# RWKV scan: inverted blocks in a 64-row buffer with zeros, unit matrices in turn, another order of the pair work

## Chip, cores, metric

One core of a Trainium2 chip runs one program of two transformer blocks in float32. The metric is the device time of that program in microseconds (us). The change touches one stage of it, the bidirectional RWKV scan, which takes about a quarter of the time.

## What is computed

The scan keeps, for each of 16 heads and 2 directions, a 64 x 64 state `s` and walks over 512 tokens (256 of context, then 256 of the sequence):

```python
def step(s, inp):
    r_t, lw_t, k_t, v_t, a_t, b_t = inp
    sa = jnp.einsum('dbhij,dbhj->dbhi', s, a_t)
    s = s * jnp.exp(lw_t)[..., None, :] + sa[..., None] * b_t[..., None, :] + v_t[..., None] * k_t[..., None, :]
    return s, jnp.einsum('dbhij,dbhj->dbhi', s, r_t)
```

The kernel does this in 16 chunks of 32 tokens. Inside a chunk the term `sa` depends on earlier tokens of the same chunk; it is solved with the inverse of a unit triangular 32 x 32 matrix. So for every head, direction and chunk there is one 32 x 32 inverse, and then a 64 x 64 matrix that takes the state from one chunk to the next.

## The kernel before, in words

The stage is `stage_rwkv_scan`. Eight **head pairs** n = 0 to 7 (two heads e = 0, 1 of 64 channels fill the 128 partitions) pass through it in a software pipeline. `scan_order()` writes one list of items by hand; all engines walk the same list, each taking its part of each item, and each engine works strictly in that order. For i = -3 to 8 it interleaves: the chain of pair i, the solve of pair i+1, the grams of pair i+2, the readout of pair i-1, the bonus and inverse of pair i+2 and the preparation of pair i+3. `interleave` gives each group a window (lo, hi) of the period; items are spread evenly in their window and then sorted. I call the time from one chain start to the next **a period**. Tiles are named by the items:

- `el`, `gram`, `btok`: VectorE makes the scaled inputs (L1915 to L1920, six operations on 128 x 512); TensorE multiplies them to 64 x 64 grams (L1581), VectorE masks them into BG (L1968); TensorE turns the inputs to token order (L1589), ScalarE copies them out.
- `inv`: SyncE writes the grams' 32 x 32 blocks (partitions 32 to 63 and 96 to 127 of BG, columns 96 to 127) to DRAM (L1503) and reads them back with one block per partition (L1510, L1512); VectorE inverts them in 30 double operations (L1933, L1935) and a last one (L1940); SyncE writes the inverses to DRAM (L1517) and reads them back into the same place of BG (L1521).
- `atok`, `akv`, `pq`, `gr`: the solve. `atok` transposes (L1589, copy L1851). `akv` (`key_values`, L1599) multiplies 32-row blocks. `pq` (`solved`) copies four blocks through TensorE with a 32 x 32 unit matrix (L1611: partitions 0 to 31 and 64 to 95) and multiplies the inverses with the values (L1618: partitions 32 to 63 and 96 to 127, output in the same ones); ScalarE copies the bank back (L1866). `gr` (`steps_made`) first lays unit matrices (L1634) and the read vectors (L1636) into two banks, for e = 0 and then e = 1, and adds products on them (L1641).
- `chain` c = 0 to 16: per chunk L1660, L1653, L1668, L1677 on TensorE, then one VectorE operation (L1987) that scales the state U for the next chunk. Chunk 1 of a pair also waits until VectorE has summed the pair before (L1999, L2000; item `read` 0).
- `kk`, `lora`, `scan`, `exps`: the preparation of pair i+3. `kk` 0 starts with a square on ScalarE (L1808), whose input SyncE loads (L1487, L1488) after `bonus` of the pair before is done on VectorE (L1979).

TensorE runs each float32 matmul as two passes, so a matmul of the code has two records in the trace. The items up to the first half of a period are, before, in this order (pair 3 in the chain): el 5/0, atok 4/0, chain 0, read 0, gram 5/0, atok, exps 5/1, akv, chain 1, read 1, btok, akv, chain 2, btok, read 2, pq, el 5/1, pq, chain 3, read 3, gram 5/1, pq, btok, pq, chain 4, read 4, btok, gr, bonus, chain 5, gr.

Of the kernel before, what the change touches and what calls it, by code (L numbers as in the profile page):

```python
# [20 lines left out]
P = 128  # L21
D = 1024
T = 256
KT = D // P
# [1314 lines left out]
def scan_order():  # L1339

    order = []
    for i in range(-3, KT + 1):
        def has(n, x):
            return x if 0 <= n < KT else []
        order += interleave((0, 1, has(i, [("chain", i, c) for c in range(NCK + 1)])),
                            (0, 0.7, has(i + 1, scan_solve(i + 1))),
                            (0, 0.3, has(i + 2, scan_grams(i + 2))),
                            (0, 0.3, has(i - 1, scan_read(i - 1))),
                            (0.3, 0.36, has(i + 2, [("bonus", i + 2, j) for j in range(2)])),
                            (0.45, 1, has(i + 2, [("inv", i + 2, s) for s in range(1, LCH)])),  # L1350
                            (0.42, 1, has(i + 3, scan_ready(i + 3))))
    return order


def stage_rwkv_scan(nc, k, a, lora, kept, o):
# [14 lines left out]
    with ExitStack() as ctx:  # L1370
# [37 lines left out]
        starts, gmask, sel, half2 = sb("starts", 512), sb("gmask", 64), sb("sel", 512), sb("half2", 6)  # L1408
        cen, omka, eps = sb("cen", P), sb("omka", KT), sb("eps", 1)
# [4 lines left out]
        x_kept = [nc.dram_tensor(f"rw_{s}_kept", (P, KT * T), F32) for s in ("x", "ctx")]  # L1414
        consts, step = sem("consts"), sem("step")
# [42 lines left out]
        with nc.Block() as block:  # L1458
# [8 lines left out]
            @block.vector  # L1467
            def _(dve):
                nc.vector.memset(er.rearrange("p (c s) -> p c s", s=LCH)[:, :, LCH - 1], 1.0)
                nc.vector.memset(en.rearrange("p (c s) -> p c s", s=LCH)[:, :, LCH - 1], 1.0)  # L1470
                nc.vector.memset(eps, GN_EPS)
                kas = row(k, "rw", 0, 9 * KT).rearrange("p (n j) -> p n j", j=9)[:, :, KA]
                nc.vector.tensor_scalar(omka, kas, -1.0, 1.0, ALU.mult, ALU.add)
                nc.vector.scalar_tensor_tensor(cen, headones, -1.0 / 64, ident, ALU.mult, ALU.add)
# [4 lines left out]
        def _(sp):  # L1479
# [19 lines left out]
            for n in range(KT):  # L1499
# [18 lines left out]
                sp.wait_ge(x_out, 32 * (n + 1))  # L1518
                for d in range(2):
                    for h in range(2):  # L1520
                        sp.dma_start(BG[n % 3][d][brows(h), :, :, 96:128].rearrange("p c e t -> p (c e) t"),  # L1521
                                     blocks(mt_dram, n, d, h)).then_inc(mt_in, 16)
# [12 lines left out]
        def _(pe):  # L1535
# [68 lines left out]
            def solved(n, d, e, half):  # L1604
# [8 lines left out]
                for j in range(4):  # L1613
                    c2 = 4 * half + j
                    for h in range(2):
                        x, y = VQ[n % 2][d][brows(h), c2, e, :], KP[d][brows(h), c2, e, :]
                        both = bass.AP(x.tensor, x.offset, [list(x.ap[0]), [y.offset - x.offset, 2], [1, 64]])
                        mm = pe.matmul(out[brows(h), j * P:(j + 1) * P], BG[n % 3][d][brows(h), c2, e, 96:128], both,  # L1618
                                       start=True, stop=True)
# [3 lines left out]
            def steps_made(n, d, half):  # L1623
# [4 lines left out]
                for h in range(2):  # L1628
                    for e in range(2):
                        unit = ident[rows64(e), rows64(e)]  # L1630
                        to = outs[h][rows64(e), 0:384].rearrange("p (c v) -> p c v", c=4)
                        rt = RT[n % 2][d][rows64(e), 256 * half:256 * half + 256].rearrange("p (c h t) -> p c h t", h=2,
                                                                                           t=LCH)
                        pe.matmul(to[:, :, 0:64], unit, unit.unsqueeze(1).to_broadcast([64, 4, 64]), start=True, stop=False,  # L1634
                                  skip_group_check=True)
                        pe.matmul(to[:, :, 64:96], unit, rt[:, :, h, :], start=False, stop=False, skip_group_check=True)  # L1636
# [962 lines left out]
```

## Time and profile before

| | us |
|---|---|
| median of 3 runs | 2722.91 (2720.7 to 2728.16) |
| the profiled execution | 2720.06 |
| its span, first to last instruction | 2718.4 |
| TensorE busy | 2245.3 (83%) |
| VectorE busy | 984.4 (36%) |
| ScalarE busy | 518.1 (19%) |
| mean granted share of the TensorE clock | 0.858 |

The page cuts the span into 40 slices of 68 us; the scan lies in slices 25 to 35. The views used are the page, busy time by windows, the timelines of single engines, and the answers for single lines. In a timeline a row is a run of equal instructions: start, duration, engine, line, operation, output and inputs, tile form (rows*columns of the array, then the moving operand) and count, and in brackets the idle time before it and what ended it. The granted clock takes two values in the scan, 0.50 (1.2 GHz) and 1.00 (2.4 GHz).

### The profile page before, as it was taken

To read this page: it belongs to the slowest core of one execution; us is meant where nothing else is said; L and a number is where in the kernel's file an instruction comes from. 1 tells how busy PE (TensorE), PEld (TensorE's weight loads), DVE (VectorE), ACT (ScalarE), POOL (GpSimd) and SP (SyncE) were. 2 spreads that over 40 slices of the span, in tenths; PEclk is the share of its full clock that TensorE was granted. 3 is DMA by queue.
4 is the path that set the end of the run, shared out by engine and by line. 5 is a ranking of instruction groups with operands and counts; after the bars stand their busy time and mean duration, and the time that the engine had idled before them with its cause. 6 is when DMAs were issued, how large, how long until landed. Compare 5 with 4: busy or idle time off the path is not lost. (4 is left out here: it accounts for less than half of the span.)

```text
span 2718.4 us, 39159 instructions
## 1 busy us (share of the span) xinstructions
PE 2245.3 (83%) x16630; PEld 1735.0 (64%) x16630; DVE 984.4 (36%) x2209; ACT 518.1 (19%) x920; POOL 58.2 (2%) x85
## 2 busy tenths in 40 slices
PE   1999955798999886899859993688888889779797
PEld 0888854687888775788624442466666777536445
DVE  3224346411440372675161003544544441120253
ACT  1011022401000101100110003444444333010142
POOL 0000000000000300000000000000000000000000
PEclk9999977898999898899979995776667776689889
DMA  7465410424874321775303203111101111312100
GB/s 289 173 230 228 171 64 8 86 93 165 336 280 155 124 78 37 281 302 217 138 16 109 92 31 125 38 39 38 35 15 39 29 25 41 124 66 93 52 10 16
DMA packets 103014, 305.14 MB, mean 112 GB/s; under 512 B 71352, under 2 KB 79800, under 8 KB 85184
## 3 DMA queue, kind: packets, MB, share of 16 engines
q1 hardware_dynamic: 94384, 225.11, 24.3%
q0 software_dynamic: 8464, 77.60, 7.3%
q8 instruction: 131, 2.15, 0.3%
q14 instruction: 35, 0.29, 0.0%
HBM read 286.88 MB, written 15.80 MB: 111 GB/s over the span
## 5 line engine op out<-in xcount | busy, mean ns | idle before, releaser
L263 PE MATMUL bank<-h,ring 128*128 128x256 f32 x2944 | 646.7, 383 | 22.8 <-DVEq L967 15.3
L263 PEld LDWEIGHTS bank<-h,ring 128*128 128x128 f32 x2944 | 566.3, 193 | 104.0 <-DVEq L967 16.0
L263 PE MATMUL bank<-mixed,ring 128*128 128x512 f32 x384 | 165.0, 592 | 1.3 <-DVE mixed L1249 1.3
L877 PE MATMUL bank<-ffn_hidden,ring 128*128 128x256 f32 x704 | 152.4, 379 | 3.3 <-PEq L903 3.3
L877 PEld LDWEIGHTS bank<-ffn_hidden,ring 128*128 128x128 f32 x704 | 133.6, 190 | 22.2 <-issue 4.1
L263 PEld LDWEIGHTS bank<-mixed,ring 128*128 128x128 f32 x384 | 72.9, 190 | 93.5 <-issue 91.4
L156 DVE CUSTOM_DVE_ANT_0 next_w<-next_w,next_vec,par 128x1024 f32<-128x1024 f32 x96 | 120.1, 1279 | 11.4 <-DMA next_w<-in_mod_stream 11.4
L1987 DVE TENSOR_TENSOR rw_u<-bank,rw_lam 128x128 f32<-128x128 f32 x120 | 35.0, 291 | 236.1 <-PE bank L1660 233.1
L889 DVE SCALAR_TENSOR_TENSOR x<-bank,mod,x 128x256 f32<-128x256 f32 x24 | 10.0, 477 | 231.6 <-PE bank L877 231.6
L1668 PE MATMUL bank<-rw_gr,rw_u 64*64 64x32 f32 x960 | 80.3, 252 | 13.0 <-DVE rw_u L1987 12.9
L1581 PE MATMUL bank<-rw_xa,ring 64*64 64x64 f32 x1024 | 30.5, 305 | 72.2 <-DVE rw_xa L1920 72.2
L877 PE MATMUL bank<-y,ring 128*128 128x256 f32 x384 | 83.1, 379 | 0.8 <-PEq L679 0.8
L401 DVE COPY y<-bank 128x512 f32<-128x512 f32 x20 | 13.8, 692 | 186.2 <-PE bank L263 186.2
L877 PEld LDWEIGHTS bank<-y,ring 128*128 128x128 f32 x384 | 72.9, 190 | 10.9 <-issue 1.1
L2087 PE MATMUL bank<-mla_h,ring 128*128 128x256 f32 (+1 forms) x240 | 67.3, 444 | 12.5 <-PEq L190 12.5
L1581 PEld LDWEIGHTS bank<-rw_xa,ring 64*64 64x64 f32 x1024 | 27.6, 212 | 75.6 <-DVE rw_xa L1920 74.5
L1090 DVE SCALAR_TENSOR_TENSOR cv_v<-cv_u,par,cv_v 128x256 f32<-128x256 f32 x150 | 67.4, 483 | 22.1 <-DVE cv_v L1090 21.0
L1668 PEld LDWEIGHTS bank<-rw_gr,rw_u 64*64 64x64 f32 x960 | 66.5, 172 | 13.9 <-issue 13.5
L1677 PE MATMUL bank<-ring 64*64 64x32 f32 x768 | 69.4, 261 | 0.5
L1660 PE MATMUL bank<-rw_u,rw_gr 64*64 64x64 f32 x896 | 61.8, 270 | 8.3 <-DVE rw_u L1987 5.6
L2087 PEld LDWEIGHTS bank<-mla_h,ring 128*128 128x128 f32 x240 | 46.6, 195 | 33.1 <-issue 28.1
L962 ACT ACTIVATE ffn_gate<-bank 128x512 f32<-128x512 f32 x22 | 13.1, 597 | 286.0 <-PE bank L263 286.0
(387 smaller groups left out, 3415.1 us busy)
## 6 DMA issues: line engine op xcount, KB each, us to landing
ring<-in_stream SPq DMA_DIRECT2D x89, 2048.0 KB, 8.0
next_w<-in_mod_stream POOLq DMA_DIRECT2D x24, 2048.0 KB, 9.9
ctx<-in_mod_rest POOLq DMA_DIRECT2D x16, 1024.0 KB, 7.3
rwkv_projections<-proj_out POOLq DMA_DIRECT2D x8, 1024.0 KB, 6.7
y<-bias_table SPq DMA_DIRECT2D x48, 128.0 KB, 4.9
rw_rkv<-rwkv_projections SPq DMA_DIRECT2D x8, 768.0 KB, 4.2
rw_at<-rw_at_kept SPq DMA_DIRECT2D x16, 256.0 KB, 3.9
rwkv_o<-rwkv_projections POOLq DMA_DIRECT2D x1, 2048.0 KB, 16.0
```

What stands on the lines that cost most here:

```text
L156: return nc.vector.tensor_tensor_reduce(products, w, vec, 1.0, bias, ALU.mult, ALU.add, out)
L263: mm = pe.matmul(out, ring_tile(k, n, kt, i * P), rhs[kt], start=start and kt == kts[0], stop=stop and kt == kts[-1])
L401: nc.vector.tensor_copy(dst, k.psum[2 * (j % 2)].rearrange("p (i t) -> p i t", i=2)).then_inc(stored_dve, 1)
L877: mm = pe.matmul(k.psum[grp * 4 + i][:, 0:T], ring_tile(k, n, kt, i * P), rhs[part * KT + kt], start=(part == 0 and kt == 0), stop=(part = ...
L962: nc.scalar.activation(gate[:, j % 2, :], k.psum[2 * (j % 2)][:], ACT.Silu).then_inc(gated, 1)
L1090: nc.vector.scalar_tensor_tensor(v[:, i:i + 1, :], u[:, i:i + 1, bass.ds(t * U + j, T)], k.par[:, bass.ds(t * U + (PAR["dw"] + i * (TAPS + ...
L1581: mm = pe.matmul(outs[e][rows64(c % 2), 64 * (c // 2):64 * (c // 2) + 64], BK[rows64(e), c].rearrange("p k s -> p (k s)"), both, start=Tru ...
L1660: mm = pe.matmul(k.psum[c % 2][rows64(e), 64 * d:64 * d + 64], GR[n % 2][d][rows64(e), c, 0:64], U[rows64(e), c % 2, d, :], start=False, s ...
L1668: mm = pe.matmul(k.psum[2 + c % 2][rows64(e), at:at + 32], U[rows64(e), c % 2, d, :], GR[n % 2][d][rows64(e), c, 64:96], start=(d == 0), s ...
L1677: mm = pe.matmul(k.psum[2 + h][rows64(e), at:at + 32], VQ[n % 2][d][rows64(h), c2, e, :], BG[n % 3][d][rows64(h), c2, e, 64:96], start=(c ...
L1987: v.tensor_tensor(U[:, (c + 1) % 2, :, :], k.psum[c % 2][:, 0:P].rearrange("p (d v) -> p d v", d=2), lam[:, n % 4, :, c + 1:c + 2].to_broa ...
L2087: mm = pe.matmul(out, ring_tile(k, n, kt, i * P), rhs[kt], start=(kt == 0), stop=(kt == KT - 1))
```

## The change

It has four parts. (1) The inverses come back from DRAM into a buffer of their own, LM, in which the partitions 0 to 31 and 64 to 95 are zeros, written once; L1618 then multiplies 64 rows (a tile of 64 x 32) in place of 32. SyncE waits for all `pq` of the pair before it writes LM. (2) In `gr` the unit matrices are fed for e = 0 and e = 1, then the read vectors for both. (3) `scan_order` has other windows. (4) The mask and `cen` move into constants that this stage no longer needs otherwise, which makes room for LM.

```diff
-                            (0, 0.7, has(i + 1, scan_solve(i + 1))),
-                            (0, 0.3, has(i + 2, scan_grams(i + 2))),
+                            (0, 0.75, has(i + 1, scan_solve(i + 1))),
+                            (0.1, 0.42, has(i + 2, scan_grams(i + 2))),
                             (0, 0.3, has(i - 1, scan_read(i - 1))),
-                            (0.3, 0.36, has(i + 2, [("bonus", i + 2, j) for j in range(2)])),
-                            (0.45, 1, has(i + 2, [("inv", i + 2, s) for s in range(1, LCH)])),
-                            (0.42, 1, has(i + 3, scan_ready(i + 3))))
+                            (0.42, 0.46, has(i + 2, [("bonus", i + 2, j) for j in range(2)])),
+                            (0.55, 1, has(i + 2, [("inv", i + 2, s) for s in range(1, LCH)])),
+                            (0.48, 0.9, has(i + 3, scan_ready(i + 3))))
...
+                for d in range(2):
+                    for h in range(2):
+                        nc.vector.memset(LM[d][krows(h)].rearrange("p a b t -> p (a b t)"), 0.0)
...
+                if n:
+                    sp.wait_ge(pq_up, 8 * n)
...
-                        sp.dma_start(BG[n % 3][d][brows(h), :, :, 96:128].rearrange("p c e t -> p (c e) t"),
+                        sp.dma_start(LM[d][brows(h)].rearrange("p c e t -> p (c e) t"),
...
-                        x, y = VQ[n % 2][d][brows(h), c2, e, :], KP[d][brows(h), c2, e, :]
+                        x, y = VQ[n % 2][d][rows64(h), c2, e, :], KP[d][rows64(h), c2, e, :]
...
-                        mm = pe.matmul(out[brows(h), j * P:(j + 1) * P], BG[n % 3][d][brows(h), c2, e, 96:128], both,
-                                       start=True, stop=True)
+                        mm = pe.matmul(out[brows(h), j * P:(j + 1) * P], LM[d][rows64(h), c2, e, :], both, start=True,
+                                       stop=True)
...
+                    for e in range(2):
+                        pe.matmul(to[e][:, :, 0:64], units[e], units[e].unsqueeze(1).to_broadcast([64, 4, 64]), start=True,
+                                  stop=False, skip_group_check=True)
+                    for e in range(2):
...
+                        pe.matmul(to[e][:, :, 64:96], units[e], rt[:, :, h, :], start=False, stop=False,
                                   skip_group_check=True)
```

The new order of a period, with TensorE's items in the same words: atok 4/0, chain 0, (read 0 on VectorE), atok, chain 1, read 1, akv, (el 5/0), akv, chain 2, read 2, gram 5/0, pq, (exps 5/1), chain 3, pq, read 3, btok, pq, btok, chain 4, read 4, pq, (el 5/1), gr, chain 5, gram 5/1, gr, btok, chain 6, atok 4/1, btok, bonus, atok, chain 7, (bonus on VectorE), akv, chain 8, akv, kk 0, pq, lora, chain 9, pq, kk 1, chain 10, pq, pq, lora, chain 11, gr, kk 2, gr, chain 12 to 16.

## Rows read from the trace of the kernel before

**Rows 1.** The page: the span, and the granted clock in 40 slices.
```profile
span 2718.4 us, 39159 instructions
PEclk9999977898999898899979995776667776689889
```
**Rows 2.** Windows: one period, then stretches of it; from:to, length, busy us, clock, DMA.
```profile
2007.40:2089.30 81.90, 71.12 (x1167) 57.58 (x1166) 38.18 (x110) 32.93 (x58) 0.00 (x0) 0.69 0.15 33
2018.88:2029.82 10.94, 10.94 (x116) 9.15 (x115) 0.58 (x2) 6.38 (x12) 0.00 (x0) 0.50 0.01 1
2018.88:2039.65 20.77, 20.77 (x275) 17.08 (x274) 6.15 (x12) 8.79 (x17) 0.00 (x0) 0.50 0.01 2
2039.65:2056.72 17.07, 15.29 (x303) 12.19 (x301) 5.31 (x10) 6.11 (x12) 0.00 (x0) 1.00 0.45 111
2056.72:2066.96 10.24, 10.24 (x110) 7.75 (x112) 3.04 (x15) 3.49 (x6) 0.00 (x0) 0.50 0.01 2
```
**Rows 3.** TensorE's timeline at the head of the next period (chain 0 to chain 1).
```profile
2089.30 0.72 PE L1653 MATMUL bank<-ring 64*64 64x64 f32 x16
2095.24 1.99 PE L1581 MATMUL bank<-rw_xa,ring 64*64 64x64 f32 x64 [5.21 <-DVE rw_xa L1920]
...
2098.94 1.92 PE L1599 MATMUL bank<-ring,x 32*32 32x64 f32 x32 [0.68 <-ACT ring L1851]
```
**Rows 4.** VectorE's timeline over the same head.
```profile
2086.15 0.29 DVE L1987 TENSOR_TENSOR rw_u<-bank,rw_lam 128x128 f32<-128x128 f32 x1
2090.96 0.37 DVE L1940 TENSOR_SCALAR rw_x<-rw_x 64x16 f32<-64x16 f32 x2
2094.49 0.69 DVE L1920 SCALAR_TENSOR_TENSOR rw_xa<-rw_kk,rw_ee 128x512 f32<-128x512 f32 x1
2096.66 0.42 DVE L2000 TENSOR_TENSOR rw_ysb<-rw_ysb,bank 128x256 f32<-128x256 f32 x1
```
**Rows 5.** TensorE's timeline: other idle times of a period, kk 2, and the tail.
```profile
2046.99 1.13 PE L1706 MATMUL bank<-ring,con 128*128 128x512 f32 x2 [0.84 <-DVE ring L1973]
2056.65 1.84 PE L1553 MATMUL bank<-rw_half,rw_bb 128*128 128x2 f32 x8 [0.26 <-ACT rw_bb L1808]
2079.26 1.15 PE L1559 MATMUL bank<-rw_kstT,rw_sel 8*128 8x128 f32 x8
2082.86 0.69 PE L1660 MATMUL bank<-rw_u,rw_gr 64*64 64x64 f32 x8 [0.82 <-DVE rw_u L1987]
2086.59 0.49 PE L1668 MATMUL bank<-rw_gr,rw_u 64*64 64x32 f32 x5 [2.23 <-DVE rw_u L1987]
```
**Rows 6.** Timelines: bonus (VectorE), square (ScalarE), last readout operation, exponents; then L1488's landing.
```profile
2048.75 0.68 DVE L1979 TENSOR_TENSOR rw_bonv<-bank,rw_rkv 128x512 f32<-128x512 f32 x1
2055.88 0.72 ACT L1808 ACTIVATE rw_bb<-rw_rkv,par 128x512 f32<-128x512 f32 x1
2044.80 0.75 DVE L2012 SCALAR_TENSOR_TENSOR rwkv_o<-rw_ycs,par,rwkv_o 128x512 f32<-128x512 f32 x1
2098.78 0.62 ACT L1791 COPY rw_xa<-rw_rkv 128x512 f32<-128x512 f32 x1
2102.38 0.80 ACT L1798 ACTIVATE ring<-rw_av,rw_omka,par 128x512 f32<-128x512 f32 x1
DMA to landing us min/median/max: 4.2/5.0/7.9
```
**Rows 7.** TensorE's timeline: a pq at the low clock, then one at the full clock.
```profile
2062.11 0.63 PE L1611 MATMUL bank<-ring,con 32*32 32x256 f32 x2
2062.12 0.64 PE L1618 MATMUL bank<-ring 32*32 32x128 f32 x4
2069.69 0.41 PE L1611 MATMUL bank<-ring,con 32*32 32x256 f32 x2
2069.94 0.82 PE L1618 MATMUL bank<-ring 32*32 32x128 f32 x12
```
**Rows 8.** TensorE's timeline: transposes, then the unit matrices of gr, at the full clock.
```profile
2043.18 0.66 PE L1589 MATMUL bank<-con,ring 128*128 128x128 f32 x4
2043.76 0.66 PE L1634 MATMUL bank<-con 64*64 64x256 f32 x4
```
**Rows 9.** TensorE's timeline: the first gram in the two periods that fill the pipeline.
```profile
1718.19 1.99 PE L1581 MATMUL bank<-rw_xa,ring 64*64 64x64 f32 x64 [16.72 <-DVE rw_xa L1920]
1777.61 1.99 PE L1581 MATMUL bank<-rw_xa,ring 64*64 64x64 f32 x64 [13.45 <-DVE rw_xa L1920]
```

More of the change, by code:

```diff
@@ L1407, in stage_rwkv_scan @@
         U, lam = sb("u", 2, 2, 64), sb("lam", 4, 2, NCK)
-        starts, gmask, sel, half2 = sb("starts", 512), sb("gmask", 64), sb("sel", 512), sb("half2", 6)
-        cen, omka, eps = sb("cen", P), sb("omka", KT), sb("eps", 1)
+        starts, gmask, sel, half2 = sb("starts", 512), const(k, "tri")[:, 0:64], sb("sel", 512), sb("half2", 6)
+        cen, omka, eps = const(k, "neg"), sb("omka", KT), sb("eps", 1)
         kst, kstT, rst, rstT = sb("kst", 8), sb("kstT", P), sb("rst", 8), sb("rstT", P)
@@ L1414, in stage_rwkv_scan @@
         x_kept = [nc.dram_tensor(f"rw_{s}_kept", (P, KT * T), F32) for s in ("x", "ctx")]
+        LM = [sb(f"lm{d}", 8, 2, LCH) for d in range(2)]
         consts, step = sem("consts"), sem("step")
@@ L1628, in steps_made @@
                 for h in range(2):
+                    to = [outs[h][rows64(e), 0:384].rearrange("p (c v) -> p c v", c=4) for e in range(2)]
+                    units = [ident[rows64(e), rows64(e)] for e in range(2)]
                     for e in range(2):
-                        unit = ident[rows64(e), rows64(e)]
-                        to = outs[h][rows64(e), 0:384].rearrange("p (c v) -> p c v", c=4)
+                        pe.matmul(to[e][:, :, 0:64], units[e], units[e].unsqueeze(1).to_broadcast([64, 4, 64]), start=True,
+                                  stop=False, skip_group_check=True)
+                    for e in range(2):
                         rt = RT[n % 2][d][rows64(e), 256 * half:256 * half + 256].rearrange("p (c h t) -> p c h t", h=2,
                                                                                            t=LCH)
-                        pe.matmul(to[:, :, 0:64], unit, unit.unsqueeze(1).to_broadcast([64, 4, 64]), start=True, stop=False,
+                        pe.matmul(to[e][:, :, 64:96], units[e], rt[:, :, h, :], start=False, stop=False,
                                   skip_group_check=True)
-                        pe.matmul(to[:, :, 64:96], unit, rt[:, :, h, :], start=False, stop=False, skip_group_check=True)
                 for j in range(4):
```

## The prediction

> **What bounds the kernel now.** I read the page first, then busy time by windows, then the timelines of TensorE, VectorE and ScalarE over one period. The page says that the clock of TensorE is near full in most of the program but 0.6 to 0.7 in the slices of the scan [rows 1]. The windows then show one period: 81.90 us, of which TensorE is busy 71.12 us and VectorE only 38.18 us [rows 2]. So TensorE is the bound, with 10.8 us idle, and it is slowed by its clock: between chain 1 and chain 7 it works 20.77 us at clock 0.50 (1.2 GHz), then 17.07 us at 1.00 (2.4 GHz), then 10.24 us at 0.50 again [rows 2]. The periods of pairs 2 to 5 are alike within 0.1 us; those of pairs 0 and 1 have larger gaps at their start [rows 9]. Five periods (chain of pairs 0 to 4) have all the groups of the list in them, so a change per period counts five times, and the rest is worked out apart.
>
> Most of the 10.8 us lies in four places. At the head of a period TensorE waits 5.21 us for VectorE's inputs of the first gram, and 0.68 us for ScalarE's copy before akv [rows 3]; before the bonus 0.84 us, before kk 0 0.26 us [rows 5]; the second akv has the same 0.68 us; and at the tail chain 14 and 15 wait 0.82 and 2.23 us for VectorE [rows 5], which is busy there with inverse and scans. At that head VectorE itself is never idle: after the state of chunk 15 (2086.15) it ends the inverse at 2091.33, the gram's inputs at 2095.18, and the sum of the readout at 2097.08 [rows 4].
>
> **Part 1: the order.** *Head.* Chain 1 comes 2098.94 + 1.85 = 2100.79 today, 14.6 us after the state of chunk 15 was scaled [rows 3, 4]. In the new list VectorE does, after the inverse (2091.33), the state of chunk 1 (0.3) and the readout sum (1.6), then chain 1 may start at about 2093.3, some 7.2 us after 2086.15. TensorE does the second atok before it; gram (1.92), first akv (1.85 and its wait of 0.68) come later, which are 4.45 us that it still has to do, less the wait. So the gain is 14.6 - 7.2 - 4.6 = 2.8 us. The waits before the bonus and the second akv go, since chain steps or transposes now stand between: 0.8 and 0.7 us. The gram's inputs, now made under akv, akv and chain 2, are no longer late.
>
> *Tail.* kk 2 (1.08 us of progress, [rows 5]) stood between chain 12 and 13. VectorE's work between the states of chunks 13 and 15 stays at 7.4 us or so (four inverse steps and a scan each), so without kk 2 TensorE only idles longer: +1.1 us.
>
> *New waits.* (a) kk 0. The load for it is released by the bonus on VectorE, which moves from before chain 5 to behind chain 7. Today the bonus operation ends at 2049.43, 1.4 us after its chain step starts, and the square runs at 2055.88 with the landing median 5.0 us after issue [rows 6]. So kk 0 can start 1.4 + 0.5 + 5.0 + 0.7 = 7.6 us after chain 7 starts at worst, about 7.3 by the spacing of the earlier pairs; TensorE has chain, akv, chain, akv in between, 4.1 us at the full clock, 7.4 us at the low one. Stalls 3.2 us instead of 0.26: +2.9 us. Behind it stand pq and lora on TensorE. (b) The second gram. VectorE now does the three readout operations (2.2 us, the last in [rows 6]) before the six inputs (4.1 us; they end at 2095.18, [rows 4]), both after read 4 on TensorE, which meanwhile has only pq, gr and chain 5, 4.5 us: +1.7 us at the full clock, none at the low one. (c) ScalarE's exponents take 2098.78 to 2103.18 = 4.4 us [rows 6] and now stand between two pq copies; the second btok needs the bank of the second: 0 to 1 us, I take 0.8. Sum of the order without clock: -2.8 - 1.5 + 1.1 + 2.9 + 1.7 + 0.8 = +2.2 us per period. By itself the new order is no gain.
>
> **Part 2: the padded blocks.** A pq today runs its two kinds of matmul side by side: at the low clock L1618 starts 0.01 us after L1611, though that takes 0.63 us a pass, and the whole block costs 1.86 us, at the full clock 1.01 [rows 7]. That works as they use different partitions. The padded L1618 uses partitions 0 to 127, so also those of L1611, though other output columns. Lower bound: it still runs beside, 0 us. Upper bound: L1618 waits for both passes of L1611, 2 x 0.43 at the low clock (2 x 0.24 at the full one) plus a change of form, for which the nearest row is four transposes, 0.11 us apart: the next form starts 0.58 us after the first, not 0.44, so about 0.1 [rows 8]. That makes +0.5 at the full clock and +1.0 at the low one; with six blocks at full and two at low, 5.0 us per period, of which 1.4 us fill waits (b) and (c): +3.6. No row has two forms at work at once, which speaks for the upper end; the row in which both kinds overlap speaks for the lower [rows 7]. I take the middle, +1.8, and keep both ends. The Trainium skill has a rule that speaks against the change: "TensorEngine Tiling (Array Packing)", Tiling Modes, says that a switch of the tiling mode, not only of the tile, drains the array. By it the sum would go to the upper end; the trace agrees in that a new form starts late [rows 8].
>
> **Part 3: the clock.** At the low clock a pq costs 1.86 us, at the full one 1.01 [rows 7]. What TensorE did before the clock rose at 2039.65: the second gram (64-row tiles, four of them), then pq; before 2066.96: pq and lora with 64 x 128 tiles. In between, with 32-row pq, akv, chain steps and the small sums, it stayed at 0.50 though TensorE was busy all the time [rows 2]. In the new order the first gram follows chain 2 and read 2 without idle time and is followed by padded pq, so I expect the rise after it, not after the second. Low-clock work from chain 1 to there: 10.94 us today up to the first pq [rows 2], less two btok (2.1), plus the second akv and the gram (1.85 + 1.92): 12.6, plus one pq. The second low stretch becomes kk 0 and a pq, some 4.7 us. Against 20.77 + 10.24 + 3.8 (gram and akv, moved in) = 34.8 now, 20.3: 14.5 us fewer at the low clock; such work takes 1/1.8 of the time at full, so -6.4 us per period. Bounds: 0 if nothing lifts it, -8.5 if the second low stretch goes as well.
>
> **Part 4: no cost.** Unit matrices in turn: today the four passes of L1634 already span 0.66 us for two halves, and at 256 columns a pass of one half takes 0.21, so two passes of both halves side by side take 0.43 plus the end of the last; both halves are at work together [rows 8]. Gain 0 to 0.1 us for each of 32 gr; I take 0. The memsets (four, at most 0.7 us) lie beside the loads of constants. The wait of SyncE for pq of the pair before: those end long before the inverse does; behind it only the return of the inverses is queued.
>
> **Sum.** Per period 2.2 + 1.8 - 6.4 = -2.4 us, five times: -12. The period of pair 5 (no kk): -3. The filling periods: TensorE stood idle 16.72 and 13.45 us before the first gram [rows 9]; atok and two akv now go into the first (5.4 us, until the first pq waits for the inverses: -3.6), and the second gains 1 us more than a later one. Last periods: padded pq against an earlier clock, 0. Total -19.6, on the profiled 2720.06: 2700.5; the median of the runs is 2.9 us higher, so **2703 us**, 0.7% less.
>
> **Rivals.** *A. The padded blocks run beside the copies.* Then -4.2 per period, and the low clock of pair 6's period is shortened as well (-5): -21 - 5 - 4.6 - 5 = -36, and up to -10 more if the clock is kept at kk 0: 2676 to 2687, say 2682. For it: other output columns. Chance 0.22. *B. The drain of the skill's rule in full, as priced from [rows 7, 8].* 2.2 + 3.6 - 6.4 = -0.6 per period, +4 in the pairs around, -4.6 at the start: -4, so 2719. Chance 0.18. *C. Slower.* The clock stays low through the first direction. Then the gain of 6.4 is gone, six pq at the low clock and two at full pay 7.0, waits (b) and (c) vanish: -4.3 + 1.1 + 2.9 + 7.0 = +6.7 per period, +33 in all, with start and end +32: 2755. It decides at the first gram and the pq behind it: is 1.00 granted before chain 4? For it: today a gram (1.99 us) at the head of the period is followed by 25 us at 0.50. Against it: it came after 5.21 us of idle time [rows 3]. Chance 0.20. *Forecast:* 0.40.
>
> **Numbers.** The range goes to A's low end and some more below, and part of the way to C: 2660 to 2738. A measurement of this kernel tells about 0.3% (8 us) from none. Faster: the forecast nearly whole (0.37), A (0.22): 0.59. Within: B and the rest of the forecast, 0.20. Slower: C and a little, 0.21.
>
> **What would show it.** Head: the wait before chain 1 about 3 us, none before the first gram. A row L1553 with 2 to 3.5 us of idle time before it. In pq, the start of L1618 against L1611: 0.01 us (A) or 0.5 us and more (B). The clock of the 20 us after chain 1: rise some 15 us in. Period 79 to 80 us. The forecast fails if the load is not late, if ScalarE becomes what TensorE waits for, or if the clock rises only with the second gram.

## The result, and the profile after

The changed kernel takes 2730.61 us (median of 20 runs, 2724.92 to 2736.34), the kernel before 2720.76 us in the same comparison. The ratio is 1.0036, with a 95% interval of 1.0027 to 1.0045: slower by 0.36% or 10 us, just beyond the 0.3% that the prediction called none. The forecast was 2703 us, and faster. The time lies within the stated range, but on the other side of the kernel before.

The profiled execution took 2728.41 us, 8.35 us more than the one of before. The page of the changed kernel, its span and the granted clock in slices (compare [rows 1]: in the scan, slices 28, 29 and 32 to 34 went up):

```profile
span 2726.8 us, 39174 instructions
PEclk9999977998999898999979995777867887689889
```

Busy time by windows, the columns of [rows 2]: the period of pair 3, then its low-clock stretch after chain 1, the full-clock stretch, and the low-clock stretch behind it.

```profile
2018.48:2101.17 82.69, 68.44 (x1167) 52.16 (x1167) 38.20 (x110) 33.88 (x58) 0.00 (x0) 0.79 0.16 32
2022.57:2037.81 15.24, 15.24 (x220) 12.29 (x222) 5.87 (x11) 3.81 (x6) 0.00 (x0) 0.50 0.19 30
2037.81:2065.10 27.29, 24.39 (x517) 19.07 (x513) 10.88 (x20) 12.53 (x24) 0.00 (x0) 1.00 0.31 65
2065.10:2075.40 10.30, 6.90 (x39) 3.99 (x41) 0.63 (x4) 4.19 (x6) 0.00 (x0) 0.50 0.09 30
```

The mean granted clock went from 0.69 to 0.79, and TensorE is busy 68.44 us instead of 71.12 [rows 2]. Yet the period is 0.8 us longer. So the change did bring the clock that it was forecast to bring, and paid more than that for it. TensorE's timeline of the same period shows where: the head (compare [rows 3]), the first gram, a block of `pq` at the full clock, the second btok and the second gram, kk 0, a block of `pq` at the low clock (compare [rows 7]), and the tail (compare [rows 5]).

```profile
2018.48 0.72 PE L1661 MATMUL bank<-ring 64*64 64x64 f32 x16
2022.57 0.55 PE L1668 MATMUL bank<-rw_u,rw_gr 64*64 64x64 f32 x5 [2.32 <-DVE rw_ysb L2008]
...
2033.58 1.99 PE L1587 MATMUL bank<-rw_xa,ring 64*64 64x64 f32 x64
...
2039.15 0.62 PE L1617 MATMUL bank<-ring,con 32*32 32x256 f32 x4
2039.70 1.06 PE L1624 MATMUL bank<-ring,rw_lm 64*32 64x128 f32 x16
...
2043.71 0.63 PE L1595 MATMUL bank<-con,ring 128*128 128x128 f32 x4 [0.76 <-ACT ring L1874]
...
2052.56 1.16 PE L1587 MATMUL bank<-rw_xa,ring 64*64 64x64 f32 x64 [1.23 <-DVE rw_xa L1928]
...
2068.50 1.87 PE L1559 MATMUL bank<-rw_half,rw_bb 128*128 128x2 f32 x8 [4.22 <-ACT rw_bb L1816]
2070.30 1.06 PE L1617 MATMUL bank<-ring,con 32*32 32x256 f32 x4
2071.29 1.92 PE L1624 MATMUL bank<-ring,rw_lm 64*32 64x128 f32 x16
...
2094.64 0.45 PE L1668 MATMUL bank<-rw_u,rw_gr 64*64 64x64 f32 x8 [2.58 <-DVE rw_u L1995]
...
2098.45 0.50 PE L1676 MATMUL bank<-rw_gr,rw_u 64*64 64x32 f32 x5 [2.92 <-DVE rw_u L1995]
```

The head: 2.32 us before chain 1 and none before the gram, in place of 5.21 and 0.68. A `pq`: L1624 starts 0.55 us after L1617 (2039.70 - 2039.15) at the full clock and 0.99 us after it at the low one, where L1618 started 0.01 us after L1611 at the low clock [rows 7]. All four passes of the two copies end first, then the 16 passes of the eight products run. The two numbers are the same in all 58 of the 64 blocks that lie wholly at one clock. From the start of the copies to the start of what follows, a block takes 1.54 us at full and 2.84 us at low clock (the full width 0.55 + 1.06 less the 0.07 us by which neighbours overlap), before 1.01 and 1.86.

TensorE's idle time and its low-clock time per period, as a mean over the periods of pairs 1 to 4, worked out from the same timelines, in us:

| | period | TensorE busy | idle | granted 0.50 |
|---|---|---|---|---|
| before | 81.90 | 71.13 | 10.77 | 51.2 |
| after | 82.97 | 68.58 | 14.38 | 35.2 |

So 16.0 us per period were moved from the low clock to the full one, busy time fell by 2.55 us only, and idle time rose by 3.6: kk 0 +4.24, tail +2.3, second gram +1.23, second btok +0.76, against -5.1 at the head and before akv and bonus. The four periods give +4.3 us of the 8.35. The first period, which also has all groups, gives +4.8 (84.7 against 79.9), the filling +3.0 (chain 0 of pair 0 at 1766.72 instead of 1763.68). The last two periods and what follows them give 3.7 back (-0.5 and -0.7 for the periods of pairs 5 and 6).

Why kk 0 is late is read on three engines. First VectorE's timeline, the bonus that releases the loads:

```profile
2060.79 0.68 DVE L1987 TENSOR_TENSOR rw_bonv<-bank,rw_rkv 128x512 f32<-128x512 f32 x1
```

Then SyncE's own queue, the last of the reads of the inverse's inputs and the two loads:

```profile
2059.34 0.60 SPq L1516 DMA_DIRECT2D rw_x<-rw_at_kept  x1
2061.56 0.34 SPq L1491 DMA_DIRECT2D rw_rkv<-rwkv_projections  x1
2061.94 0.57 SPq L1492 DMA_DIRECT2D rw_w<-in_lora_out  x1
```

ScalarE's timeline, the square:

```profile
2067.72 0.72 ACT L1816 ACTIVATE rw_bb<-rw_rkv,par 128x512 f32<-128x512 f32 x1 [2.81 <-DMA rw_w<-in_lora_out]
```

And the answer for line L1492, from issue to landing in all 8 pairs:

```profile
DMA to landing us min/median/max: 5.2/5.8/7.2
```

The bonus ends at 2061.47, the loads are issued at 2061.56 and 2061.94, the second lands 5.76 us later, and the square starts at once. TensorE has nothing between 2064.3 and 2068.50. The clock also falls in this wait, at 2065.10, and stays down for the 10.30 us of the last window. The load that ScalarE waits for is the one for the lora weights, which the square doesn't use: the wait is on both loads at once.

The bonus is not the only thing that holds the loads back. SyncE issues them behind the reads of the inverse's inputs, in one queue. In the period of pair 2 the bonus ended at 1976.41, and the load followed the last of these reads. SyncE's queue there:

```profile
1976.24 0.60 SPq L1516 DMA_DIRECT2D rw_x<-rw_at_kept  x1
1977.02 0.52 SPq L1491 DMA_DIRECT2D rw_rkv<-rwkv_projections  x1
```

This is the period in which kk 0 waits longest, 5.96 us.

The filling periods, TensorE's timeline of the changed kernel (compare [rows 9]):

```profile
1707.58 3.62 PE L1605 MATMUL bank<-ring 32*32 32x64 f32 x64 [8.07 <-ACT ring L1859]
1715.90 1.99 PE L1587 MATMUL bank<-rw_xa,ring 64*64 64x64 f32 x64 [4.70 <-DVE rw_xa L1928]
1719.30 1.06 PE L1617 MATMUL bank<-ring,con 32*32 32x256 f32 x4 [1.41 <-DMA rw_lm<-rw_mt_kept]
...
1747.22 1.87 PE L1559 MATMUL bank<-rw_half,rw_bb 128*128 128x2 f32 x8 [7.16 <-ACT rw_bb L1816]
```

The akv did move into the idle time before the first gram, but that gram starts at 1715.90 instead of 1718.19 [rows 9], where VectorE's inputs set it; and kk 0 of pair 2 waits 7.16 us, 1.30 us before the change.

### The profile page after: what moved, and what is told of

Read it like the earlier page. It is cut to its first block and busy times, and to the rows that moved or that the text cites. A ratio compares the mean times of both kernels' runs of the same rounds, so it can differ in the third digit from the quotient of the medians.

```text
span 2726.8 us, 39174 instructions
## 1 busy us (share of the span) xinstructions
PE 2240.8 (82%) x16630; PEld 1706.8 (63%) x16630; DVE 986.8 (36%) x2213; ACT 521.4 (19%) x924; POOL 58.2 (2%) x85
## 5 line engine op out<-in xcount | busy, mean ns | idle before, releaser
L1676 PE MATMUL bank<-rw_gr,rw_u 64*64 64x32 f32 x960 | 74.5, 242 | 15.3 <-DVE rw_u L1995 15.2
L1668 PEld LDWEIGHTS bank<-rw_u,rw_gr 64*64 64x64 f32 x896 | 42.1, 158 | 71.8 <-issue 64.8
L1624 PEld LDWEIGHTS bank<-ring,rw_lm 64*32 64x32 f32 x1024 | 58.4, 121 | 36.9 <-issue 33.6
L1624 PE MATMUL bank<-ring,rw_lm 64*32 64x128 f32 x1024 | 81.2, 307 | 0.0
L1676 PEld LDWEIGHTS bank<-rw_gr,rw_u 64*64 64x64 f32 x960 | 61.0, 160 | 16.1 <-issue 15.8
```

What stands on the lines that cost most here:

```text
L1624: mm = pe.matmul(out[brows(h), j * P:(j + 1) * P], LM[d][rows64(h), c2, e, :], both, start=True, stop=True)
L1668: mm = pe.matmul(k.psum[c % 2][rows64(e), 64 * d:64 * d + 64], GR[n % 2][d][rows64(e), c, 0:64], U[rows64(e), c % 2, d, :], start=False, s ...
L1676: mm = pe.matmul(k.psum[2 + c % 2][rows64(e), at:at + 32], U[rows64(e), c % 2, d, :], GR[n % 2][d][rows64(e), c, 64:96], start=(d == 0), s ...
```

## The experiments

Each kernel was compared with the kernel before on the same chip. The theories at the outset: **F**, the change of tile form inside a block makes L1624 wait for L1617; **S**, not the form but the shared partitions make it wait; **L**, the late loads behind the bonus cost the gain; **O**, the order is a loss by itself. Ratios are to the kernel before, with the 95% interval.

**1. The padded blocks alone (e1_pad_only).** Old windows, old order in `gr`:

```diff
-                            (0, 0.75, has(i + 1, scan_solve(i + 1))),
-                            (0.1, 0.42, has(i + 2, scan_grams(i + 2))),
+                            (0, 0.7, has(i + 1, scan_solve(i + 1))),
+                            (0, 0.3, has(i + 2, scan_grams(i + 2))),
...
```

> The kernel before with the padded blocks alone (LM buffer, 64-row L1618, the wait for pq before LM is written), old order, old gr. Theory (the padded block waits for the copies' passes and a change of form): a pq takes 1.54 us at the full clock and 2.84 us at the low one, as in the changed kernel, against 1.01 and 1.86 before; +4 to +5 us per period, of which an earlier rise of the clock gives back some; 2720 to 2740 us. Rival (the padding is free and lifts the clock, the loss is the order's): faster than before, 2700 us or less.

Measured: 2721.7 us, ratio 1.0007 (0.9998 to 1.0016). Period 80.79 us, low-clock time 34.7 us against 51.2, blocks at 1.54 and 2.84 us. The time lies in the range of the theory, but the period is 1.1 us shorter and not longer. In this one profile the low-clock time falls from 42.5 to 26.6 us over the four periods; steadier is the mean granted clock of whole runs, 0.872 to 0.877 in all 11 against 0.850 to 0.867 in the 76 runs of the kernel before that were made beside the experiments. So the clock rises by the padding without any new order, and the longer blocks eat it.

**2. The order alone (e2_order_only).** The kernel before with the six new windows.

> The kernel before with the new windows of the order alone; blocks of 32 rows, old gr. Theory: the same waits as in the changed kernel (2.3 us before chain 1, 0.8 before the second btok, 1.2 before the second gram, about 4 before kk 0), pq at 1.01 us; the clock rises later than in the changed kernel, since the first gram is followed by 32-row blocks. 2715 to 2735 us. Rival (the order alone lifts the clock, the padding only costs): clock rises within 16 us after chain 1, 78 us per period, 2705 us or less.

Measured: 2734.56 us, ratio 1.0058 (1.0041 to 1.0075). Period 85.57, low-clock time 54.0: the new order doesn't lift the clock, and costs 14 us. Its waits are near those of the changed kernel: chain 1 2.32, kk 0 3.95 in the mean (2.4 to 6.4), chain 14 and 15 2.58 and 2.35. The second gram waits 1.72 us in two of the four periods and not at all in the other two, and the second btok does not wait.

**3. The turn alone (e3_turn_only), and the same kernel again (e3_turn_again).**

```diff
-                        pe.matmul(to[:, :, 0:64], unit, unit.unsqueeze(1).to_broadcast([64, 4, 64]), start=True, stop=False,
+                        pe.matmul(to[e][:, :, 0:64], units[e], units[e].unsqueeze(1).to_broadcast([64, 4, 64]), start=True,
...
```

> The kernel before with the unit matrices fed to both halves in turn alone. Theory: both halves were at work together before; 0 to -0.1 us for each of 32 gr, so 2718 to 2721 us. Rival (they were serial): -0.4 us each, -13 us.

> The unit matrices in turn alone, once more, for a second profile. Its times fell into two groups, 2707 to 2714 and 2735 to 2743 us. Theory (the same work, locked in two ways to the changes of the clock): a profile of either group has the same durations at each clock and the same waits, and differs in the time spent at the low clock; in the slow group a period takes 3.4 us more or twice that. Rival (contention for memory or a late load): a wait appears in the slow group that the other has not.

Measured: 2726.98 us (12 runs, from 2706.61 to 2742.77), ratio 1.0027 (0.9995 to 1.0058); again, 2730.76 us (5 runs), ratio 1.0049 (1.0027 to 1.007). Neither is the 2718 to 2721 us of the theory. Of the first 12 runs five lie at 2707 to 2714 and seven at 2727 to 2743, with nothing between. Windows over the period of pair 3, of a profiled run of the first group, then of one of the second:

```profile
2003.43:2081.93 78.50, 66.68 (x1167) 53.92 (x1166) 38.21 (x110) 32.83 (x58) 0.00 (x0) 0.74 0.17 34
```
```profile
2004.99:2086.91 81.92, 70.89 (x1167) 57.49 (x1166) 38.20 (x110) 32.95 (x58) 0.00 (x0) 0.69 0.15 33
```

The same instructions, with the same waits (0.4 us more at each of chain 14 and 15 in the first), but at clock 0.74 and 0.69. Each repeats its period over pairs 1 to 4 within 0.03 us. That the other runs of a group have the same rhythm as its profiled one is inferred from their times alone, and no run of this kernel above 2728 us was profiled. The turn itself is worth some 0.05 us per `gr`: at the full clock it takes 2.29 to 2.32 us before, from its start to the start of what follows, and 2.23 to 2.27 with the turn.

**4. One form of tile in the block (e4_one_form).** The changed kernel, with the copy multiplying 64 rows too; the unit matrix has zeros in the rows of the inverse, so its result is the same:

```diff
-                              ident[krows(h), krows(h)], VQ[n % 2][d][krows(h), at, e, :], start=True, stop=True)
+                              ident[rows64(h), krows(h)], VQ[n % 2][d][rows64(h), at, e, :], start=True, stop=True)
```

> The changed kernel, but the four copies of pq also take 64 rows (a 64 x 32 slice of the unit matrix), so that both kinds of matmul in a pq have the same tile form, with other output columns. Theory (the change of form makes L1624 wait): without it they run side by side, pq near 1.05 us at full and 1.9 us at the low clock, some -4 us per period, 2705 us. Rival (the shared partitions make it wait): pq stays at 1.45 us and more, 2726 us or more.

Measured: 2703.72 us, ratio 0.9939 (0.9926 to 0.9952). TensorE's timeline, a block at the full clock and the start of one at the low clock:

```profile
2033.76 0.41 PE L1617 MATMUL bank<-ring,con 64*32 64x256 f32 x2
2033.78 0.41 PE L1624 MATMUL bank<-ring,rw_lm 64*32 64x128 f32 x4
2034.00 0.38 PE L1617 MATMUL bank<-ring,con 64*32 64x256 f32 x2
2034.02 0.82 PE L1624 MATMUL bank<-ring,rw_lm 64*32 64x128 f32 x12
```
```profile
2030.08 0.64 PE L1617 MATMUL bank<-ring,con 64*32 64x256 f32 x2
2030.09 0.64 PE L1624 MATMUL bank<-ring,rw_lm 64*32 64x128 f32 x4
```

Copies and products now read all the same partitions, and still L1624 starts 0.01 or 0.02 us after L1617. The block costs 1.01 and 1.86 us, as before the change. F holds, S falls: the row range of one matmul's operands is worth 27 us. What stays untested is whether two forms would run side by side if they also read different partitions.

**5 to 7. The loads earlier.** The lora weights (L1492) are loaded a pair ahead and the first two planes of rkv before the bonus; only the third plane stays behind it, with a semaphore of its own. On the changed kernel (e5_early_load), on the one with one form (e6_one_form_early), and on the kernel before with the new order (e8_order_early):

```diff
-                    sp.wait_ge(lora_up, 2 * n)
-                    sp.wait_ge(bon_down, n)
-                sp.dma_start(rkv, kept[n, :, 0:3, :]).then_inc(loaded, 16)
-                sp.dma_start(w2, a["lora_out"][:, :, n * P:(n + 1) * P]).then_inc(loaded, 16)
+                sp.dma_start(rkv[:, 0:2, :], kept[n, :, 0:2, :]).then_inc(loaded, 16)
+                if n >= 1:
+                    sp.wait_ge(bon_down, n)
+                sp.dma_start(rkv[:, 2, :], kept[n, :, 2, :]).then_inc(v_loaded, 16)
+
+            def load_w(n):
+                if n >= 1:
+                    sp.wait_ge(lora_up, 2 * n)
+                sp.dma_start(w2, a["lora_out"][:, :, n * P:(n + 1) * P]).then_inc(loaded, 16)
...
```

> The changed kernel with the load that kk 0 waits for taken apart: L1492's weights a pair ahead, the first two thirds of L1491 without the wait for the bonus, the last third behind it. Theory (the late bonus makes kk 0 wait about 4 us, the first cost of the new order): the wait before kk 0 falls to 1.3 to 2.5 us, some -2 to -3 us per period and more in the filling periods (7 and 8 us there), so -12 to -20 us against the changed kernel: 2710 to 2718 us, just under the kernel before. Rival (the stall only takes the place of other idle time or of low-clock time): no change, 2728 to 2732 us.

> Both mends: one tile form in pq and the load taken apart. Theory (two separate costs, both on TensorE's path): they add up, 2704 - 12 to 20 = 2684 to 2692 us. Rival (they share idle time or clock): 2698 to 2706 us, as with one form alone.

> The new order alone, 32-row blocks, with the load taken apart. Theory (the order costs by its stalls, most by that of kk 0): 2734 falls by 12 to 20 us to 2714 to 2722 us, near the kernel before; the clock stays low longer than in the changed kernel. Rival (the order costs by the clock, not by the load): 2728 us or more.

Measured: 2724.05 us, ratio 1.0016 (1.0002 to 1.0031); 2697.27 us, ratio 0.9922 (0.9893 to 0.9951); 2728.94 us, ratio 1.0036 (1.0018 to 1.0055). That is 6.6, 6.4 and 5.6 us less than the same kernels without it, about half of the 12 to 20 us of the theories; only the first is clear of the noise, as the intervals of the others overlap with those of the kernels without it. The third time lies in the range of its rival. The wait before kk 0 falls from 4.5 to 3.3, from 4.8 to 3.3 and from 3.95 to 1.8 us per period. Why it does not go is seen in SyncE's queue, here of e5_early_load:

```profile
2060.15 0.60 SPq L1524 DMA_DIRECT2D rw_x<-rw_at_kept  x1
2060.86 0.67 SPq L1489 DMA_DIRECT2D rw_rkv<-rwkv_projections  x1
```

The load no longer waits for the bonus (which ends at 2062.35) but follows the last read of the inverse's inputs by 0.7 to 0.8 us, as it does for every pair but the first in all three kernels. These reads wait for the second gram, which the new order also moved. Issued ahead of the reads the load could go earlier; no run tried it. L is a part of the loss, some 6 of the 9 to 14 us that the order costs.

**8. One form, old order (e7_one_form_old_order), and with the turn (e9_one_form_turn).** The edit of experiment 4 on the kernel of experiment 1, and the same with the turn.

> The padded blocks with one tile form, in the old order and with the old gr. Theory (padding without the change of form is free and the clock rises earlier): pq 1.0 us at full and 1.9 at the low clock, low-clock time per period some 12 us shorter than before, 2695 to 2705 us. Rival (the clock gain came from the new order, not from the padding): 2715 to 2722 us.

> Padded blocks with one tile form in the old order, and the unit matrices in turn. Theory (the turn gains 0.04 us per gr, as its rows in the changed kernel say, and otherwise only moves where the clock changes fall): 2688 to 2696 us, the same as without it, perhaps with two groups of times. Rival (the turn costs, as its median alone seemed to say): 2698 us or more.

Measured: 2692.53 us, ratio 0.9901 (0.9877 to 0.9924); 2691.55 us, ratio 0.9894 (0.9879 to 0.9909). The good part of the change, taken alone, is worth 1%: the blocks cost what they did before the change, and low-clock time falls from 51.2 to 41.0 us per period. Not all of that is owed to the zero rows: the first group of experiment 3 has none and stands at 40.9 us in a period of 78.49, against 78.54 here. But this kernel is 19 us faster than that group (medians 2692.5 and 2711.8), in the first period (74.2 against 81.6 us) and in that of pair 6 (52.3 against 60.0). The new order costs 11 us of it (2703.72 in experiment 4). The turn adds nothing that can be told. O holds with all three kinds of block: the new order costs 14, 9 and 11 us (table below).

**9. Another order (e10_gram_later), and with the early loads (e11_gram_later_early).** From the kernel e7_one_form_old_order, the grams are moved only a little and the bonus stays near its place:

```diff
-                            (0, 0.3, has(i + 2, scan_grams(i + 2))),
+                            (0.07, 0.34, has(i + 2, scan_grams(i + 2))),
...
-                            (0.3, 0.36, has(i + 2, [("bonus", i + 2, j) for j in range(2)])),
+                            (0.34, 0.37, has(i + 2, [("bonus", i + 2, j) for j in range(2)])),
...
-                            (0.42, 1, has(i + 3, scan_ready(i + 3))))
+                            (0.45, 1, has(i + 3, scan_ready(i + 3))))
```

> Padded blocks with one form, old gr, and the old order but for the grams at 0.07 to 0.34, the bonus at 0.34 to 0.37 and the preparation from 0.45: chain 1 before the first gram, but the bonus before chain 6. Theory (of the new order the head is a gain and the late bonus and readout are the loss): 2.3 us of waiting before chain 1 in place of 5.2 and 0.7, no wait before kk 0 over 0.5 us, up to 1 us before the second gram; 3 us per period less, 2675 to 2685 us. Rival (idle time at the head is paid back at the tail or by the clock): 2690 to 2700 us.

> The kernel with the grams at 0.07 to 0.34 and also the load taken apart. Theory (kk 0 does not wait for the load there): the same within 3 us. Rival (it still does, above all in the filling periods): 5 us or more below it.

Measured: 2656.23 us, ratio 0.9767 (0.9754 to 0.9781); 2649.78 us, ratio 0.9744 (0.9731 to 0.9758). Both beat both kernels. The first is 19 us below even the low end of its theory: the waits at the head shrink to 1.4 us, but kk 0 waits 1.6 in place of at most 0.5, and what the text had not reckoned with is the clock, with low-clock time of 25.5 us per period of 71.53. With the early load the rival holds, 6.5 us less, but hardly at the kk 0 of the full periods, where the wait falls only from 1.6 to 1.3: the square there follows ScalarE's copy of the second akv without idle time, so no load is late. The kk 0 of pair 2, in the filling, waits 1.37 us in place of 4.15, and chain 0 of pair 0 comes 4.3 us earlier.

**10. That order with the other two kinds of block (e12_two_forms_gram_later, e13_short_rows_gram_later).** The copy with 32 rows again (the first edit of experiment 4 undone); and the kernel before, with the three windows of experiment 9.

> Order of the kernel with the grams a little later (2656 us with one form of tile), blocks of the changed kernel with their two forms. Theory 'a form change is paid in every block': 128 blocks of 0.53 us at the full clock, as in the old order where the pair of kernels stood 29 us apart, so 2656 + 30 = about 2685. Rival 'the idle times hide it': this order has little idle time behind the blocks, but VectorE's head and tail waits could absorb some; then 2665 to 2675. Rival 'the clock follows': if the form change also takes the clock down in the middle of a period, 2695 or more.

> The same order on the kernel before, with its 32-row blocks and no padding. Theory 'padding lifts the clock': low-clock time per period stays near 45 to 50 us in place of 25.5, so at 1.8 times the work a period of 79 to 81 us and 2700 to 2715 in all. Rival 'the order alone does it': no wait before the first gram and a clock that rises after it, as with padding: period near 72 us, 2660. What decides is the granted clock between chain 1 and chain 4.

(The 128 blocks of the first text should read 64: eight pairs of eight; at 0.53 us they are 34 us.) Measured: 2703.74 us, ratio 0.9937 (0.9908 to 0.9965); 2716.24 us, ratio 0.9957 (0.9934 to 0.9981). The first is 47.5 us slower than with one form, more than 34: "the clock follows". The second is 1 us above the range of its theory and 56 above its rival; its low-clock time (36.7 us) and period (76.0 us) lie between the two, and its periods are uneven, from 72.7 to 80.9 us. With the others this fills a table of medians, which is the shortest statement of what the parts do:

| us | order of before | order of the change | order of experiment 9 |
|---|---|---|---|
| 32-row blocks | 2720.8 | 2734.6 | 2716.2 |
| padded, two forms | 2721.7 | 2730.6 (with turn) | 2703.7 |
| padded, one form | 2692.5 | 2703.7 (with turn) | 2656.2 |

Down a column, the second form costs 29, 27 and 48 us. Along a row, the order of the change costs 14, 9 and 11 us, and that of experiment 9 gives 5, 18 and 36 us. Order and padding each give little alone and 65 us together.

Windows show what they share. The kernel e10_gram_later: the period of pair 3, and the part of it up to the rise of the clock; then the same two of e12_two_forms_gram_later:

```profile
1982.14:2053.54 71.40, 61.19 (x1167) 49.81 (x1166) 38.13 (x110) 32.86 (x58) 0.00 (x0) 0.83 0.19 37
1982.14:1993.46 11.32, 9.92 (x163) 7.55 (x164) 7.99 (x23) 4.75 (x8) 0.00 (x0) 0.50 0.32 48
```
```profile
2007.13:2084.27 77.14, 69.94 (x1167) 52.78 (x1166) 38.13 (x110) 33.25 (x58) 0.00 (x0) 0.79 0.17 35
2007.13:2026.76 19.63, 18.23 (x246) 14.21 (x246) 9.35 (x26) 11.57 (x19) 0.00 (x0) 0.50 0.23 35
```

Both do the same instructions in the same order up to the first gram and the second akv, and the first `pq` comes only after these. Yet the clock rises 11.3 us after chain 0 in one, before its first `pq`, and 19.6 us after chain 0 in the other. So the reason can't lie in what TensorE does in these 11 us alone, but in what came before: in e10_gram_later the clock had fallen 5.7 us before chain 0 (at 1976.40), in e12_two_forms_gram_later 7.6 us before it (at 1999.50). The 48 us are the form change itself, 34 us or more, and a clock that falls into another rhythm with it (33.7 us at the low clock per period in place of 25.5). What sets the moment of a rise is not settled by these runs.

Between e10_gram_later and e13_short_rows_gram_later, which differ in the padded blocks only (with the buffer and the wait that belong to them), low-clock time per period is 25.5 and 36.7 us, and the period of pair 6 takes 52.1 and 73.4 us. Over all runs the mean granted clock is 0.883 to 0.887 with the padding and 0.855 to 0.865 without: here its share stands by itself.

## Where the prediction was right, and where it was wrong

**The size of the padded blocks.** This is the step that failed first: part 2 took +1.8 us per period, and +5.0 were measured. The bounds were 0 and +0.5 us (full) or +1.0 us (low) per block, and the middle was taken, because no row of before had two forms at work at once and one row had both kinds of matmul side by side. The upper bound was the measured value: +0.53 and +0.98 us. That the two kinds overlap today because they use different partitions was wrong: they overlap as well on the same ones, if they have one form (experiment 4). The change of form was the right cause. In the period of pair 3 the eight blocks take 14.69 us; at the same clocks in one form they would take about 1.7 + 6 x 1.01 + 1.86 = 9.6 (the first stands at both clocks). That is 5 us per period, not 1.8, and little hides it: of the waits it was to fill, gram and btok kept 1.23 and 0.76 us though the long blocks stand before them. Rows that show a resource free for two instructions of one form say nothing on two forms; the two ends should not have been averaged. The trace of before could have decided it. From 1760 to 2300 us its TensorE timeline has 283 places where the form changes without idle time between, of 21 kinds, and in none does the second matmul start more than 0.07 us before the end that the profile gives the first; of neighbours with one form, 97% overlap by more than 0.16 us. The Trainium skill ("TensorEngine Tiling (Array Packing)", Tiling Modes) has the rule that changing the mode, not only the tile, drains TensorE. The trace agrees, with 0.55 and 0.99 us from the start of L1617 to that of L1624 with two forms, and 0.02 and 0.01 with one. Rival B, built on this, put the time at 2719, 12 us short of the measured; what it lacked is in the next points. Nor is the block the whole error: with one form the cost of the blocks is gone, and the kernel takes 2704 us, where rival A had 2682.

**kk 0.** The mechanism was right and the term too small: 3.2 us against 4.5 (3.7 to 6.0). From chain 7 to kk 0 I took 7.3 of at worst 7.6 us; it was 8.4 (2060.09 to 2068.50). The landing had been taken at the median of before, 5.0 us [rows 6]. It is 5.8 us now, behind the four reads of the inverse's inputs, which are issued just before (the last at 2059.34). That the reads cause the longer landing is argued, not shown. What was missed is that the clock falls in this wait, and that the load stands behind these reads in SyncE's queue: where most of it is taken out from behind the bonus, the wait falls by no more than 1.2 to 2.1 us (experiments 5 to 7).

**Tail.** +1.1 us was forecast; measured are +2.3 in the mean, +2.45 in the period of pair 3 (2.58 + 2.92 less 0.82 + 2.23 [rows 5]). VectorE's timeline, the states of two chunks of the changed kernel, then the first of the same two before the change (the second, at 2086.15, is in [rows 4]):

```profile
2090.32 0.29 DVE L1995 TENSOR_TENSOR rw_u<-bank,rw_lam 128x128 f32<-128x128 f32 x1 [0.76 <-PE bank L1668]
...
2098.01 0.29 DVE L1995 TENSOR_TENSOR rw_u<-bank,rw_lam 128x128 f32<-128x128 f32 x1
```
```profile
2078.76 0.29 DVE L1987 TENSOR_TENSOR rw_u<-bank,rw_lam 128x128 f32<-128x128 f32 x1 [1.16 <-PE bank L1660]
```

VectorE takes 7.69 us between them, before 7.39: "7.4 us or so" was right within 0.3, but by luck: before, these 7.39 us held one scan, 0.75 us of kk 2 and an idle time of 0.94 us, and now a second scan (1.23 us) and an eighth double step of the inverse stand in their place. kk 2's 1.08 us were counted. What was not: chain 13 and 14 now run at the full clock, 1.17 and 0.89 us in place of 1.64 and 1.49, and since VectorE sets the pace there, those 1.07 us turn into idle time. 1.08 + 0.30 + 1.07 = 2.45. A gain by the clock is none where TensorE waits anyway; the clock term should have left the tail out.

**Filling.** This is the second step that failed, and it weighs as much. Up to chain 0 of pair 0 the forecast was -3.6 us, for the period of pair 0 it was -3.4 (1 us more than for a later one); measured are +3.0 and +4.8. The step said that work moved into the idle time before the first gram is a gain. It is one only if the gram was not waiting for something of its own: it was, for VectorE, and the gain was the 2.3 us seen above, lost again at the kk 0 of pair 2 (7.16 us, 1.30 before) and of pair 3 (4.23 us, 0.34 before).

**Order as a whole.** The head's sum has a slip: 4.45 us "less the wait" are 3.8 and not 4.6, which makes a gain of 3.6 us in place of 2.8, and 3.6 is what was measured (5.21 + 0.68 less 2.32). Terms that were right: 2.32 us of wait before chain 1 for "about 3"; no wait before the first gram; the waits before bonus and akv gone; second gram 1.23 us for 1.7; second btok 0.76 us for 0.8. The text said that by itself the new order is no gain (+2.2 us per period). Measured alone it is +3.7 per period (experiment 2: 85.57 against 81.90) and 14 us in all.

**Clock.** Right: the clock rises 15.2 us after chain 1 (2022.57 to 2037.81), "some 15 us" was said, and before chain 4. The low-clock time falls by 16.0 us per period, 14.5 were forecast. Priced as the forecast priced it (work at the low clock takes 1.8 times as long), that is 16.0 x 0.44 = 7.1 us for the 6.4 forecast. Rival C, in which the clock stays low, is out. But the cause was put in the wrong place: it was to come from the new order and the padding together, but the order alone leaves 54.0 us at the low clock and the padding alone 34.7.

**Turn and mask.** Both were costed at nothing. With the padded blocks in one form the turn changes nothing that can be told (experiment 8). Alone, on the kernel before, its 17 runs have a median of 2728.6 us, with the 0.05 us per `gr` gained and the clock in one of two rhythms; whether the turn makes the slower one more likely stays open. The mask was not tested by itself.

The forecast's per-period sum, with measured terms: idle time +3.6, blocks +5.0, clock -7.5 (what is left of busy -2.55 behind the blocks), makes +1.1. The forecast had +2.2 + 1.8 - 6.4 = -2.4. So of the 3.5 us between them 3.2 are the blocks and 1.4 the waits, and the clock gave 1.1 back. Over the whole program the profiled time is 28 us above the forecast for it (2728.41 and 2700.5): 14 us are in the four periods of pairs 1 to 4, 15 in the filling and the period of pair 0, 2.5 in the period of pair 5, and the end gives 3 back.

Two smaller readings: the periods that are alike are those of pairs 1 to 4 (that of pair 5 takes 70.68 us), and the larger gaps of [rows 9] stand before chain 0 of pair 0 and in its period. The 2.9 us that were added for the median came from three runs; with 20 it is 0.7.

## What to carry to other kernels

Before a matmul of a short tile gets more rows, look which matmuls of another kind run beside it: give all that stand interleaved the same form, by zeros if need be, or they run one after the other. A part that pays only through the clock is to be measured alone and with its neighbours: here order and padding gave 5 and 28 us apart and 65 together. If a load's release is moved later, count from its release to the engine that waits on it, with the landing time of a busy queue, split the load if only a part of it needs the release, and look what stands before it in its queue: the wait that ends last may be that one.

## What was not expected of the hardware

Two forms of tile on different output columns don't work at the same time, 64\*32 beside 32\*32, though no idle time shows in the trace: the loss is only the overlap, 0.53 us of a 1.54 us block. The same holds for all the 335 changes of form without idle time that the changed kernel's timeline has from 1760 to 2300 us, but for five, from a tile of 128\*8 to one of 128\*128. Zero rows lift the clock: in the order of experiment 9 TensorE stands 25.5 us per period at 1.2 GHz with them and 36.7 us without, for the same items in the same order. And a loop can lock to the clock's changes in more than one way: one program gave periods of 78.5 and of 81.9 us, each steady over four pairs, in profiled executions of 2708.62 and 2727.97 us. A 0.5% comparison of such kernels needs many runs, and a difference of that size between two profiled executions may be no effect of the edit at all.
